# Sixteen groups of down projections: the weight loads move from SyncE's queue to ScalarE's, and two hand-written schedules take other sizes

## The reference, cut to what matters

```
def block(args):                       # for each token t: 8 heads x 16 chosen experts
    tb, eb, gb = args
    u = jnp.take(expert_u, eb, axis=0)
    act = jax.nn.gelu(jnp.einsum('ted,td->te', u, tb)) * gb
    vv = jnp.take(expert_v, eb, axis=0)
    return jnp.einsum('te,ted->td', act, vv)
```

## Time and profile before

| | |
|---|---|
| median of three runs | 3960.4 us |
| profiled execution, its own time | 3964.08 us |
| its span in the trace | 3962.5 us |
| TensorE busy | 3813.3 us (96%) |
| VectorE busy | 2704.9 us (68%) |
| ScalarE busy | 1219.4 us (31%) |
| GpSimd busy | 1406.9 us (36%) |
| chain that ended last: TensorE, VectorE, DMA | 49%, 11%, 7% |

### The profile page before, as it was taken

How to read it: one execution, slowest core, us unless ns; L and a number is a source line. 1 busy time by engine, 2 the same in 40 slices (tenths; PEclk the granted TensorE clock), 3 DMA queues, 4 the chain that set the end, 5 groups by cost and what they waited for, 6 DMA issues and landing times.

```text
span 3962.5 us, 53089 instructions
## 1 busy us (share of the span) xinstructions
PE 3813.3 (96%) x19109; PEld 3268.4 (82%) x19109; DVE 2704.9 (68%) x3547; ACT 1219.4 (31%) x1299; POOL 1406.9 (36%) x921
## 2 busy tenths in 40 slices
PE   8999999999999999999999999999999889899997
PEld 5888777787788788888888887777889889899997
DVE  7565888559532755454767665777885777788895
ACT  4333222344322322222333332222223333322222
POOL 1100000332211344545000055888553434456653
PEclk9999999999999999999999999999999999999999
DMA  4565555665753555455777777777877999888994
GB/s 171 191 220 166 164 168 168 221 218 174 245 204 117 183 172 185 165 186 190 232 250 256 255 249 245 263 265 249 304 266 270 342 337 351 318 337 337 350 352 169
DMA packets 272219, 941.22 MB, mean 238 GB/s; under 512 B 37793, under 2 KB 83889, under 8 KB 194633
## 3 DMA queue, kind: packets, MB, share of 16 engines
q1 hardware_dynamic: 94448, 446.73, 31.2%
q0 software_dynamic: 71504, 283.37, 20.7%
q10 hardware_dynamic: 106176, 210.00, 16.8%
HBM read 893.10 MB, written 238.31 MB: 286 GB/s over the span
## 4 chain that ended last, share of the span: by engine, by line
PE 49%; DVE 11%; DMA 7%; POOL 4%; issue 4%; ACT 3%; SPq 0%; ACTq 0%; DVEq 0%; POOLq 0%
PE mm L2134 13%; PE mm L2135 12%; PE mm L2136 12%; DMA raw<-stream 5%; DVE wlo L1239 4%; DVE acc L2034 3%; POOL gv L705 2%; POOL el L698 2%; PE pv L2134 2%; PE pv L2136 2%; PE pv L2135 2%; ACT whi L788 2%; DMA gl<-up_d 1%; PE sc L2134 1%; PE sc L2135 1%
## 5 line engine op out<-in xcount | busy, mean ns | idle before, releaser
L1239 DVE TENSOR_TENSOR wlo<-raw,whi 128x2048 fp32r<-128x2048 f32 x329 | 755.9, 2298 | 480.0 <-ACT whi L788 440.3
L788 ACT ACTIVATE whi<-raw 128x2048 fp32r<-128x2048 f32 x378 | 723.5, 1914 | 449.6 <-issue 194.5
L2134 PE MATMUL mm<-t_hi,whi 128*128 128x512 f32 x2048 | 804.2, 393 | 34.8 <-DVE wlo L1239 28.9
L2135 PE MATMUL mm<-t_lo,whi 128*128 128x512 f32 x2048 | 800.4, 391 | 0.0
L2136 PE MATMUL mm<-t_hi,wlo 128*128 128x512 f32 x2048 | 799.6, 390 | 0.0
L2034 DVE SCALAR_TENSOR_TENSOR acc<-gv,ac,acc 128x2048 f32<-128x2048 f32 x254 | 596.3, 2348 | 80.1 <-DMA gv<-ev_d,idx_v 66.6
L2134 PEld LDWEIGHTS mm<-t_hi,whi 128*128 128x128 f32 x2048 | 386.4, 189 | 124.2 <-issue 26.0
L2136 PEld LDWEIGHTS mm<-t_hi,wlo 128*128 128x128 f32 x2048 | 386.3, 189 | 81.3
L2135 PEld LDWEIGHTS mm<-t_lo,whi 128*128 128x128 f32 x2048 | 386.5, 189 | 77.6
L744 POOL DMA_INDIRECT gv<-ev_d,idx_v x128 | 244.5, 1910 | 432.6 <-DVE acc L2034 359.8
L2134 PE MATMUL mm<-hn_hi,whi 128*128 128x512 f32 x960 | 377.6, 393 | 8.2 <-DVE wlo L1239 8.2
(11 more groups left out here) (476 smaller groups left out, 7346.1 us busy)
## 6 DMA issues: line engine op xcount, KB each, us to landing
raw<-stream SPq DMA_DIRECT2D x380, 1024.0 KB
ev_d<-stream ACTq DMA_DIRECT2D x128, 1024.0 KB
up_d<-sgl ACTq DMA_DIRECT2D x128, 256.0 KB
g_d<-gst ACTq DMA_DIRECT2D x12, 2048.0 KB
spill<-stage ACTq DMA_DIRECT2D x44, 256.0 KB, 2.0
gg<-g_d SPq DMA_DIRECT2D x28, 384.0 KB
gl<-up_d SPq DMA_DIRECT2D x56, 192.0 KB
gl<-up_d SPq DMA_DIRECT2D x72, 128.0 KB
```

The costliest lines, as they stand in the source:

```text
L788: act.activation(whi[:, k, :], raw[:, k, :], ACT.Copy).then_inc(hi_done, 1)
L1239: dve.tensor_tensor(wlo[:, k, :], raw[:, k, :], whi[:, k, :].bitcast(F32), ALU.subtract)\
L2134: pe.matmul(out, lh, rh, start=start, stop=False)
L2135: pe.matmul(out, lh, rl, start=False, stop=False)
```

## The change

The weight loads of the down stage from unit 2 on are taken out of SyncE's queue. ScalarE issues them itself, behind each `split_hi` of the stage, once that unit's low half is done. The slots are spread over the groups as 6, 6, 6, 6, 7, 7, 7, 7, then six times 12, then 4 (before: eight times 7, four times 11, twice 12, then 4). `lead` follows with 12 (before: 14). The gate quarters are issued in steps 2, 4, 6 and 7 (before: 1, 3, 5, 7), and all wait for the gate product of step 0 only.

```
-SLOTS2 = _counts(SLOTS, (7, G1 - 1), (11, 4), (12, 2), (4, 1))
+SLOTS2 = _counts(SLOTS, (6, 4), (7, 4), (12, 6), (4, 1))
+GATE_STEPS = (2, 4, 6, 7)
 # SyncE
-            load_down(0, 2)
             for g in range(GROUPS_D - 1):
                 for v in range(8):
-                    u = 8 * g + v + 1
-                    if u > 2:
-                        load_down(u // 8, u % 8)
...
-                    if v % 2 == 1 and g + 2 < GROUPS_D:
-                        sp.wait_ge(gated_done, 8 * g + 8 + v)
+                    if v in GATE_STEPS and g + 2 < GROUPS_D:
+                        sp.wait_ge(gated_done, 8 * g + 9)
...
-            for v in range(1, 8):
-                load_down(GROUPS_D - 1, v)
 # GpSimd
-            lead = SLOTS2[1][0] + SLOTS2[1][1]
+            lead = 2 * SLOTS2[1][1]
 # ScalarE
+            def next_weights(u):
+                if u < 8 * GROUPS_D:
+                    act.wait_ge(hi_done, U_DOWN + u - 1)
+                    act.wait_ge(lo_done, U_DOWN + u - 1)
+                    act.dma_start(raw[:, u % 2, :], a["stream"][U_DOWN + 8 * (u // 8) + 4 * (u % 2) + u % 8 // 2])\
+                        .then_inc(raw_in[u % 2], 16)
+            next_weights(2)        # ahead of the stage, behind the last act_high of the stage before
             def down_hi(g, v):
...
                 split_hi((U_DOWN + v + 1) // 2 + 4 * g, (v + 1) % 2)
+                next_weights(8 * g + v + 3)
```

More of the change, by code:

```diff
@@ L422, in _ @@
                         sp.dma_start(gg[:, 1, 0:TE // 32, :], gg_src[1][:, 0:TE // 32, :]).then_inc(gn_in, 16)
-                    if v % 2 == 1 and g + 2 < GROUPS_D:
-                        sp.wait_ge(gated_done, 8 * g + 8 + v)
+                    if v in GATE_STEPS and g + 2 < GROUPS_D:
+                        sp.wait_ge(gated_done, 8 * g + 9)
                         nb = (BLOCKS if g + 2 >= G1 else TE // 32) // 4
-                        ns = slice(nb * (v // 2), nb * (v // 2) + nb)
+                        piece = GATE_STEPS.index(v)
+                        ns = slice(nb * piece, nb * piece + nb)
                         sp.dma_start(gg[:, g % 2, ns, :], gg_src[g + 2][:, ns, :]).then_inc(gn_in, 16)
```

## The result

The changed kernel takes 3975.51 us (median of 6 runs, 3970.28 to 3981.46), the kernel before 3961.0 us in the same series (6 runs, 3957.93 to 3965.11): a ratio of 1.0031, 95% interval 1.0019 to 1.0043. It is slower by 8 to 17 us (the medians differ by 14.5), against a forecast of +12.0. The profiled execution took 3970.7 us, near the fastest of the six; its span is 3969.2, only 6.7 us over the span before.

What follows compares the result with a forecast made beforehand. It took DMA loads to bound groups 1 to 8 and TensorE, with VectorE close behind, groups 9 to 14. -30.9 + 0 + 42.9 = +12.0 us on 3960.4 gave 3972.4 us, range 3942 to 4000.

Steps and rivals of the forecast that it cites:

- the likeliest case: Whole kernel: first half at 350 GB/s, late numbers stall `weights` in the second; +12.0 us, 3972.4 us, chance 0.42.
- the landing: Groups 9 to 14: a batch's last number lands 8.3 us after the rows ahead of it start to be issued.
- Weight loads and bytes, first half: Groups 1 to 8: loads leave at once, 143.6 MB move at 350 GB/s in 410.3 us; -30.9 us.
- rival D: Groups 1 to 8 reach group 13's 361 GB/s: -43.4 + 42.9, no change, 3959.9 us; chance 0.13.
- 1.4 us for each pair of loads: Down stage: per pair of units the load path gets some 1.4 us shorter, as neither loads nor gates wait for the other.
- Rival C: Groups 1 to 8 don't speed up beyond their bytes: -12.5 + 42.9 = +30.4, 3990.8 us; chance 0.20.
- Gates in other steps: Down stage: loads and gates no longer wait for each other; the 25.4 us of `gl` waits shrink to under 5.
- ScalarE's issues at no cost: Down stage: ScalarE's added issues of 0.33 to 0.38 us cost nothing, at most 18 us in the second half.
- The start: Before group 1: unit 2's load leaves several us later, group 0 gives some back; 0, ends -3 and +4 us.
- Twelve slots and the late number, second half: Groups 9 to 14: VectorE's slack goes and `weights` waits for its last number, 43.6 us in all; +42.9 us.
- The rule on completion order: Gather queue, groups 9 to 14: a number lands no sooner than the rows ahead of it; +42.9 us, without it +20.4.
- Rival A: Groups 9 to 14: numbers don't queue behind the rows; -30.9 + 20.4 = -10.5, 3949.9 us; chance 0.17.

Runs made afterwards that it cites:

- e8: The kernel before with the gates' new steps and wait alone (2, 4, 6, 7, all on step 0's product); 3926.6 us, ratio 0.9904.
- e3: The changed kernel with the old slots and `lead` 14, so the loads on ScalarE and the gates' new steps alone; 3927.3 us, ratio 0.9908.
- e10: The changed kernel with the row gathers for the second and third slot of each batch of 12 fetching one number a token; one run, 3959.4 us.
- e12: The kernel before with weight loads on ScalarE and gates in the old steps, all waiting for step 0's product; 3985.9 us, ratio 1.0056.

## Why the prediction was right, point by point

**Size and sign.** Forecast 3972.4, measured 3975.5. The mechanisms of the likeliest case are the ones that came, but that the total came within 3 us is luck: its two terms were both too small, by a quarter and a sixth of what was measured, and the errors (-11.4 and +8.8 us) cancel. Neither the rate (360 GB/s) nor the landing (9.2 us and more) lay in the 345 to 355 and 7.6 to 9.0 that this case was given. One sign that was named as wrong, a first half under 400 us, did appear (398.9). And the stages add up to +9.4 us, the spans to +6.7, while the timed medians differ by 14.5: the 5 to 8 us between are placed in no stage.

**Weight loads and bytes, first half.** Forecast -30.9 us at 350 GB/s; measured -42.3 at 360, the rate of rival D. The mechanism (late issues, then bytes by rate) holds: alone, the slots brought 14.0 us (12.5 by bytes) and the gates and loads 38.3. The mis-sized term is the rate; group 13's 361 GB/s was the better guess. The prediction's own 1.4 us for each pair of loads, over the 32 pairs of this half, gives 45 us as an estimate, nearer to the 36.1 (e8) and 38.3 (e3) than what it took from bytes. Rival C (no gain beyond the bytes) is out. But the part that I gave to ScalarE's queue was due to the gates' new steps and wait, as the gates' edit alone shows. The sentence of the Trainium skill ("DMA: Bandwidth & Descriptors", "Issuing engines are not separate DMA queues") that speaks against a gain from another issuing engine held; my reading of it as a case for C was wrong, since the lateness could be mended without a second queue.

**Gates in other steps.** I costed them together with the loads and said that neither would wait for the other. I did not see that the two edits need each other in one direction: the loads' move without the gates' costs 170 us. VectorE's waits for `gl` in the first half fell from 25.4 to 11.5 us, most of it in one wait of 7.6 us at the start, not under 5 as I wrote.

**ScalarE's issues at no cost.** Right in the second half: VectorE's wait between its products stayed at 0.65 us. In the first half it went from 0.54 to 0.64, since there `act_high` starts 0.1 us later behind the issue; VectorE had slack there.

**The start.** TensorE's gap before unit 2 grew from 3.8 to 6.6 us, the price I had as +3, and group 0 gave it back: from the last gate product ahead of the stage (2967.72 and 2964.94) to group 1 it is 66.7 us before and 67.3 after. The 0 stands.

**Twelve slots and the late number, second half.** Forecast +42.9, measured +51.7. Waits of 49.2 against 43.6: in groups 11 to 14 8.6 to 9.3 us (7.8 forecast), in group 10 6.8, in group 9 6.6 (4.6 forecast). The mis-sized term is the landing, 9.2 to 10.2 us from the rows' issue, not 8.3. Groups 10 to 13 took 75.6 to 76.5 us from `weights` to `weights`, forecast 74; group 14, which has no such wait at its end, took 65.3. The rest, 2.5 us, is the slack that I had at 0.7 us and that wasn't there: the kernel with twelve slots and no waits takes 403.3 against the 400.9 of my sum.

**The rule on completion order.** The Trainium skill ("DMA: Bandwidth & Descriptors", "Queues, rings and completion order") made the number land no sooner than the rows ahead. The runs agree: taking the rows away cut the waits from 49.2 to 29.8 us, and the queue's packets show the number behind the rows. Rival A had the waits at 21.1, by a landing 2.0 us after the issue that a number alone doesn't reach.

## What to carry to other kernels

When a schedule of sizes changes, follow every count derived from it to the last element that a batch waits for, and compare the event that releases that element with the moment it is due: here one lead of 12 instead of 14 ate 49 us and hid a gain of 37. An issue that waits holds everything behind it in its queue, so look first for the wait (its step and its count), and only then for another queue. And a second queue takes away an order that the first one gave for nothing: a small load that stood ahead of a large one may come last, the more so if its packets are small.

## What the runs showed of the hardware that was not expected

A gather of one number for each of 128 partitions, with no row gather issued just ahead (e10), landed 2.9 to 3.7 us after its issue ended in groups 10 to 14 and 4.5 us in group 9; behind two gathers of 1 MB (the changed kernel) it took 6.2 to 7.7 us. A `gl` load of 192 KB, issued behind 384 KB of gates in one queue and beside a weight load and gathers in two others, took 15.7 us to land (e12). In such a stretch the queues moved about as many packets each, so that the one with packets of 1.2 KB got 0.18 MB through while one with 8 KB got 1.02. The DMA engines sustained 367 GB/s over 403 us at a busy share of 0.95 (e3). Behind a standstill of 6.67 us TensorE's matmuls came at 0.32 us instead of 0.17 for 3 us (changed kernel).
